# Gathering tile 1 of a product-key layer in two halves of 64 tokens

## The reference

```python
q = (xt @ wq).reshape(T, 8, 2, 128)                      # T = 256 tokens, 8 heads
scores = einsum('thcd,hcnd->thcn', q, keys)
s_top, i_top = top_k(scores, 16)                         # per half key
cand = s_top[:, :, 0, :, None] + s_top[:, :, 1, None, :]
best, pos = top_k(cand.reshape(T, 8, 256), 16)
idx  = expert number of each of the 16 best              # 128 experts for a token
gate = softmax(best)
hid  = gelu(einsum('td,thkd->thk', xt, U[idx]))          # U: 16384 x 2048
out  = einsum('thk,thkd->td', gate * hid, V[idx])        # V: 16384 x 2048
x = rms_norm(x + out)
```

## Time and profile before

| what | value |
|---|---|
| median of three runs | 2141.59 us |
| profiled execution, its time | 2130.46 us |
| its span, first to last instruction | 2128.6 us |
| gathers of U: first and last issue | 873.5 and 1541.6 us |
| tile 1's weights begin | 1555.8 us |
| last copy of the scatter ends | 1611.4 us |
| gathers of V's columns: last issue | 2101.1 us |
| busy: PE, DVE, ACT, POOL | 69%, 76%, 41%, 46% of the span |
| DMA engines in the gather stage | 0.95 to 1.02 busy, 367 to 425 GB/s |

### The profile page before, as it was taken

The page is one execution under the profiler, slowest core; times in us unless marked ns, Lnnn a source line. Parts: engine busy times, 40 slices in busy tenths (PEclk is TensorE's granted clock), DMA queues, the critical chain, the costliest instruction groups (busy, mean ns, idle before and its releaser), DMA issues.

```text
span 2128.6 us, 26462 instructions
## 1 busy us (share of the span) xinstructions
PE 1476.9 (69%) x9809; PEld 1370.3 (64%) x9809; DVE 1614.0 (76%) x2119; ACT 870.0 (41%) x1109; POOL 973.1 (46%) x699
## 2 busy tenths in 40 slices
PE   6999999999999999920000001221358999999996
PEld 6987998898999889820000001221347999999996
DVE  4455765455644556789999989877988999999997
ACT  4353432343333444312111226567655444444443
POOL 1002220000000000168888888888867777667763
PEclk9999999999999999965555555555579999999998
DMA  5555434444554555689999999999917999999996
GB/s 190 175 180 187 154 125 139 163 145 139 178 170 168 199 181 174 254 312 422 422 419 412 421 401 407 409 417 422 420 78 249 355 359 357 361 363 358 359 355 237
DMA packets 151527, 597.80 MB, mean 281 GB/s; under 512 B 14688, under 2 KB 14704, under 8 KB 118000
## 3 DMA queue, kind: packets, MB, share of 16 engines
q0 software_dynamic: 58048, 356.02, 41.8%
q1 hardware_dynamic: 93360, 240.22, 32.0%
HBM read 594.09 MB, written 2.10 MB: 280 GB/s over the span
## 4 chain that ended last, share of the span: by engine, by line
PE 50%; issue 19%; POOL 13%; DVE 12%; DMA 4%; ACT 2%; POOLq 0%; DVEq 0%; SPq 0%; ACTq 0%; PEldq 0%
PE acc L1567 8%; PE acc L1570 8%; PE acc L1569 8%; POOL slots L489 6%; POOL starts L528 5%; DVE slots L1368 4%; PE acc L1584 3%; PE acc L1586 3%; PE acc L1585 3%; DMA slots<-in_peer_u,expert 3%; PE acc L1872 2%; PE acc L1874 2%; PE scr L1874 2%; PE acc L1873 2%; PE scr L1872 2%
## 5 line engine op out<-in xcount | busy, mean ns | idle before, releaser
L857 DVE TENSOR_TENSOR w_lo<-raw,w_hi 128x2048 fp32r<-128x2048 f32 x136 | 314.7, 2314 | 311.5 <-ACT w_hi L544 310.4
L1368 DVE SCALAR_TENSOR_TENSOR slots<-slots,acc 128x2048 f32<-128x2048 f32 x188 | 424.7, 2285 | 46.3 <-DMA slots<-in_peer_u,expert 44.2
L544 ACT ACTIVATE w_hi<-raw 128x2048 fp32r<-128x2048 f32 x136 | 260.1, 1913 | 441.5 <-PE acc L1570 295.6
L528 POOL DMA_INDIRECT starts<-in_v_gather,expert x256 | 346.5, 1353 | 150.1 <-DVE X L1508 97.7
L489 POOL DMA_INDIRECT slots<-in_peer_u,expert x256 | 252.1, 985 | 257.2 <-DVE expert L1340 148.4
L1567 PE MATMUL acc<-hT_hi,w_hi 128*128 128x256 f32 x1024 | 293.9, 287 | 3.1 <-PE acc L1570 2.6
L497 POOL TENSOR_TENSOR slots<-slots,N 128x2048 f32<-128x2048 f32 x62 | 280.5, 4525 | 32.7 <-DMA slots<-in_peer_u,expert 32.4
L1569 PE MATMUL acc<-hT_lo,w_hi 128*128 128x256 f32 x1024 | 291.8, 285 | 0.0
L1570 PE MATMUL acc<-hT_hi,w_lo 128*128 128x256 f32 x1024 | 291.6, 285 | 0.0
L830 ACT ACTIVATE v_hi<-v_raw 128x1408 fp32r<-128x1408 f32 x128 | 177.0, 1383 | 278.2 <-PE scr L1874 239.0
L739 ACT ACTIVATE slots<-slots 128x2048 f32<-128x2048 f32 x62 | 118.4, 1910 | 362.4 <-POOL slots L497 362.4
(11 more groups left out here) (278 smaller groups left out, 3336.7 us busy)
## 6 DMA issues: line engine op xcount, KB each, us to landing
raw<-in_w_in SPq DMA_DIRECT2D x88, 1024.0 KB, 4.9
v_raw<-in_v_dense SPq DMA_DIRECT2D x128, 704.0 KB, 6.2
raw<-in_w_o SPq DMA_DIRECT2D x16, 1024.0 KB, 5.0
raw<-in_peer_wq SPq DMA_DIRECT2D x16, 1024.0 KB, 5.1
raw<-in_w_a_up SPq DMA_DIRECT2D x8, 1024.0 KB, 5.0
raw<-in_w_b_up SPq DMA_DIRECT2D x8, 1024.0 KB, 5.0
slots<-in_peer_u,expert POOLq DMA_INDIRECT x256, 9.4
starts<-in_v_gather,expert POOLq DMA_INDIRECT x256, 6.3
```

The costliest lines, as they stand in the source:

```text
L528: pool.indirect_dma_start(starts[s % CRING][:, :], None, v_gather[:, :], bass.IndirectOffsetOnAxis(ap=expert[:, s // NSEL, s % NSEL:s % NS ...
L544: a.activation(w_hi[:, m % 2, :, :], raw[:, m % 2, :, :], ACT.Copy).then_inc(hi_ready, 1)
L857: v.tensor_tensor(w_lo[:, m % 2, :, :], raw[:, m % 2, :, :], w_hi[:, m % 2, :, :].bitcast(fp32), ALU.subtract).then_inc(lo_ready, 1)
L1368: v.scalar_tensor_tensor(out=slots[j][:, :], in0=slots[j][:, :], scalar=1.0, in1=row, op0=ALU.mult, op1=ALU.mult, accum_out=hid_sum[:, t, ...
```

## The change

Tile 1's 128 gathers are laid out in two phases of 64 (`PHASES` = 0, 128, 192, 256). A gather of phase 1 fetches for each of the first 64 tokens of tile 1 two of its experts, one into partition p and one into partition 64 + p; phase 2 does so for the last 64 tokens. The number of gathers and their bytes stay. What goes with it:

- SP copies the expert numbers (`expert_twice`, 16 DMAs between partitions) and doubles the tokens' vectors in `N1` (three DMAs of 512 KB).
- The sums lie in two halves of the partitions; `fold_hid` on TensorE brings them to one row for a token, through PSUM.
- `rows_to_psum`, `weights`, `turn_gate` and `copy_gate` run three times in place of two.
- 48 of the 64 scatter batches lie beside the gathers (groups 35 to 63: one for a group until 42, then 40 in 21 groups), 16 behind them. Every second batch from 8 on, and the first eight, take the gate weight on ACT.
- The row ring: gather 127 goes to DVE in place of POOL; from gather 204 on the ring has seven buffers, 6, 7, 8, 11, 12, 9, 10 in this order, three of them new.
- First one-hots behind the gathers: ten places, two made by ACT in groups 60 and 61, most by POOL.

```diff
-ROW_AT = (24, 152, 32, 40, 48, 56, 64, 72, 80, 88)
-LAST_TEN = 124
+ROW_AT = (24, 152, 32, 40, 48, 56, 64, 72, 80, 88, 112, 160, 188)
+FIRST_TEN, LAST_TEN = 10, 124
+LAST_EIGHT = 204
+LATE_ROWS = (6, 7, 8, 11, 12, 9, 10)
+PHASES = (0, NSEL, NSEL + NSEL // 2, GATHERS)
+HALF = P // 2
...
+SCATTERS = NT * BATCHES
+IN_GATHERS = SCATTERS - BATCHES // 2
...
-SPREAD_FROM, SPREAD_TWICE = 35, 57
+SPREAD_FROM, SPREAD_TWICE = 35, 43
...
-    return q % FOUR == FOUR - 1 and FOUR <= q < GATHERS - 1
+    return q % FOUR == FOUR - 1 and FOUR <= q < GATHERS - 1 and q != NSEL - 1
...
     if q < LAST_TEN:
-        return (q - FOUR) % len(ROW_AT)
-    return 2 + (q - LAST_TEN) % SLOTS
+        return (q - FOUR) % FIRST_TEN
+    if q < LAST_EIGHT:
+        return 2 + (q - LAST_TEN) % SLOTS
+    return LATE_ROWS[(q - LAST_EIGHT) % len(LATE_ROWS)]
...
+def weighted_first(n):
+    return n < IN_GATHERS and (n < ACT_WEIGHTS or n % 2 == 0)
...
-    return "dve" if n % PLACES == 7 else "act" if n % PLACES == 3 else "pool"
+    return "act" if n < AHEAD or n == 12 else "dve" if n == 9 else "pool"
...
+            def double_experts(pair):
+                sp.wait_ge(expert_ready, 4 + pair + 1)
+                ks = slice(2 * pair * TOPK, 2 * (pair + 1) * TOPK)
+                cs = slice(pair * TOPK, (pair + 1) * TOPK)
+                for u in range(2):
+                    for r in range(2):
+                        sp.dma_start(expert_twice[r * HALF:(r + 1) * HALF, u, cs].rearrange("p (h k) -> p h k", h=2),
+                                     expert[u * HALF:(u + 1) * HALF, 1, ks].rearrange(
+                                         "p (h r k) -> p h r k", h=2, r=2)[:, :, r, :]).then_inc(experts_in[pair], 16)
+            double_experts(0)
+            double_experts(1)
+            sp.wait_ge(product_ready, sum(map(on_pool, range(NSEL))))
+            for r in range(2):
+                sp.dma_start(N1[r * HALF:(r + 1) * HALF, 0, :], N1[0:HALF, 1, :]).then_inc(rows_in, 16)
+            sp.wait_ge(rows_in, 32)
+            sp.dma_start(N1[0:HALF, 1, :], N1[HALF:P, 1, :]).then_inc(rows_in, 16)
+            double_experts(2)
+            double_experts(3)
...
+                if phase:
+                    act.wait_ge(rows_in, (32, 48)[phase - 1])
+                    for q in range(PHASES[phase] - SLOTS, PHASES[phase]):
                         if not on_pool(q):
                             act.wait_ge(row_used[buffer_of(q)], uses_before(q + 1, buffer_of(q)))
...
                 if i == GROUPS // 2 - 1:
                     rows_to_psum(1)
+                if i == PHASES[2] // FOUR:
+                    rows_to_psum(2)
                 if on_pool(FOUR * i + FOUR - 1):
                     sum_product(FOUR * i + FOUR - 1)
-                if i == GROUPS // 2 + 1:
-                    weight_curves(0)
+                for w in range(NT):
+                    if i == PHASES[w + 1] // FOUR + 1:
+                        weight_curves(w)
...
             def dot(q):
...
+                phase = phase_of(q)
+                if q >= FOUR and q - PHASES[phase] >= 2:
+                    dve.wait_ge(h2_rows, 2 * phase + 2)
                     row = acc[:, :, :].rearrange("p a n -> p (a n)")
+                else:
+                    if phase:
+                        dve.wait_ge(rows_in, (32, 48)[phase - 1])
+                    row = N1[:, phase // 2, :]
...
+            def fold_hid(w):
+                pe.wait_ge(ij_ready, NT)
+                pe.wait_ge(gateT_ready, w)
+                for j in range(len(ROW_AT)):
+                    if uses_before(PHASES[w + 1], j):
+                        pe.wait_ge(row_used[j], uses_before(PHASES[w + 1], j))
+                for r in range(2):
+                    rows = slice(r * HALF, (r + 1) * HALF)
+                    to = hid_ps.rearrange("p (h r k) -> p h r k", h=H, r=2)[:, :, r, :]
+                    for u in range(w):
+                        last = t_.matmul(to, (ident if u == r else turned)[rows, :],
+                                         hid_sum[rows, 1, u * HALF:(u + 1) * HALF].rearrange("p (h k) -> p h k", h=H),
+                                         start=u == 0, stop=u == w - 1)
+                    if r == 0:
+                        last.then_inc(half_folded, 1)
+                        pe.wait_ge(half_folded, w)
+                last.then_inc(hid_landed, 1)
...
-            for n in range(BATCHES):
-                scatter(0, n)
-            turn_gate(1)
-            for n in range(BATCHES):
-                scatter(1, n)
+                if m == spread(PHASES[2] // FOUR + 1)[0]:
+                    fold_hid(1)
+                    turn_gate(1)
+                scatter(m)
+            fold_hid(2)
+            turn_gate(2)
+            for m in range(IN_GATHERS, SCATTERS):
+                scatter(m)
```

More of the change, by code:

```diff
@@ L121, in spread, with until @@
 def spread(g):
-    twice = 2 * max(0, g - SPREAD_TWICE)
-    first = max(0, min(g, SPREAD_TWICE) - SPREAD_FROM) + twice
-    return range(min(BATCHES, first), min(BATCHES, first + (g >= SPREAD_FROM) + (g >= SPREAD_TWICE)))
+    def until(g):
+        late = GROUPS - SPREAD_TWICE
+        return (max(0, min(g, SPREAD_TWICE) - SPREAD_FROM)
+                + max(0, g - SPREAD_TWICE) * (IN_GATHERS - SPREAD_TWICE + SPREAD_FROM) // late)
+    return range(until(g), until(g + 1))
+def weighted_first(n):
+    return n < IN_GATHERS and (n < ACT_WEIGHTS or n % 2 == 0)
 def parts(g):
@@ L479, in gather @@
                 t, k, j = q // NSEL, q % NSEL, buffer_of(q)
-                if k % (2 * TOPK) == 0:
+                index = expert_twice[:, k // HALF, k % HALF:k % HALF + 1] if t else expert[:, 0, k:k + 1]
+                if t == 0 and k % (2 * TOPK) == 0:
                     pool.wait_ge(expert_ready, q // (2 * TOPK) + 1)
+                if t and k < HALF and k % TOPK == 0:
+                    pool.wait_ge(experts_in[k // TOPK], 64)
+                if j == 10 and not uses_before(q, j):
+                    pool.wait_ge(product_ready, sum(map(on_pool, range(PHASES[2]))))
+                if j == 12 and not uses_before(q, j):
+                    pool.wait_ge(ij_ready, NT)
                 if q == 0:
@@ L721, in _, with rows_to_psum @@
                     hi(G_WQ + 2, m, i, 4)
-            def rows_to_psum(t):
+            def rows_to_psum(phase):
                 act.wait_ge(h2_ready, NT)
-                if t:
-                    for q in range(NSEL - SLOTS, NSEL):
+                if phase:
+                    act.wait_ge(rows_in, (32, 48)[phase - 1])
+                    for q in range(PHASES[phase] - SLOTS, PHASES[phase]):
                         if not on_pool(q):
@@ L819, in high_e @@
                 q, at0 = 2 * pair // (P // PIECES), 2 * pair % (P // PIECES)
-                for t in range(NT):
-                    last = a.activation(e_hi[:, pair % 2, t, :],
-                                        weight_of[t][q][:, at0:at0 + 2, :].rearrange("p a s -> p (a s)"), ACT.Copy)
+                a.activation(e_hi[:, pair % 2, 0, :],
+                             weight_of0[q][:, at0:at0 + 2, :].rearrange("p a s -> p (a s)"), ACT.Copy)
+                last = a.activation(e_hi[:, pair % 2, 1, :].rearrange("p (a u s) -> p u a s", a=2, u=2),
+                                    weight_of1[:, :, 2 * pair:2 * pair + 2, :], ACT.Copy)
                 last.then_inc(e_hi_ready, 1)
@@ L1836, in scatter @@
+            def scatter(m):
+                pe.wait_ge(scattered, 1 + m)
+                n = m - IN_GATHERS
+                if m < IN_GATHERS:
+                    pe.wait_ge(a_ready[0], m + 1)
                 else:
                     by = maker(n)
-                    earlier = sum(maker(m) == by for m in range(PLACES, n + 1))
-                    pe.wait_ge(a_ready[("pool", "dve", "act").index(by) + 1], earlier + (PLACES if by == "act" else 0))
-                pe.wait_ge(b_hot_ready, t * BATCHES + 1 + n)
+                    pe.wait_ge(a_ready[("pool", "dve", "act").index(by) + 1],
+                               sum(maker(e) == by for e in range(n + 1)))
+                pe.wait_ge(b_hot_ready, 1 + m)
```

257 lines of the change are left out of this document (143 added, 114 removed).

## The result

| | before | after |
|---|---|---|
| median of 20 runs | 2138.54 us (2132.71 to 2146.48) | 2148.87 us (2140.9 to 2155.33) |
| profiled execution (its span) | 2130.46 us (2128.6) | 2151.72 us (2149.9) |

The ratio is 1.0041, with a 95% interval of 1.0028 to 1.0054: slower by 0.41%, 8.8 us (6.0 to 11.5 by the interval; the two medians lie 10.3 us apart). The forecast was 8.4 us faster.

A forecast was written before the change was run, and what follows sets the result against it. It took DMA as the gather stage's bound, with the scatter tail behind it wholly on the path. Terms -23.5 + 9.8 + 0.3 + 3.75 + 1.2 = -8.4 us gave a 2133 us median, range 2118 to 2150 (forecast's own 2126 to 2139).

The forecast's parts named there:

- tail's scatter: Behind the last gather: 16 of 32 scatter batches leave the tail, which gets 23.5 us shorter.
- from product 251 to it: Between POOL's last product and the tail's scatter: fold_hid replaces the softmax part at about equal cost, difference 0.
- phase 2 begins: Around gather 204: ACT's late copy to PSUM delays DVE, then POOL, and DMA loses 9.8 us (ends 2 and 16).
- ring of seven: Late gathers: buffer reuse waits for ACT's sum with 0.7 us left; cost 0 to 2 us, taken as 0.3.
- copies of the vectors: Gather stage: three copies of 512 KB between partitions at 412 GB/s add 3.75 us of DMA time.
- tile 1 begins: Gathers 123 to 131: late doubled vectors, gather 127 on DVE, a freer dot 128; taken 0, ends -1 and +4.
- expert numbers: Gather stage: 16 DMAs in 2048 pieces of 32 B add 1.2 us; ready some 15 us before they are wanted.
- the weights before it cost the same: Before the tail's scatter: softmax part (1.55 us) goes, fold_hid (taken as 1.6 us) comes; ends -0.4 and +1.
- the distance of four: Ring at phase 2: gather 204 reuses gather 200's buffer, formerly eight apart; 7.4 us lost at gather 204.
- rival C: Vector copies touching 64 partitions run at half rate, 7.5 us in place of 3.75; total 2137 us; chance 0.15.
- A (lateness hidden): Phase 2's start: the lateness mostly doesn't reach DMA, 2 of 9.8 us stay; total 2125 us; chance 0.24.
- B (the handshake as bound): Groups from 43: ACT, TensorE and DVE wait on each other, groups outlast DMA's 10 us; 2154 us; chance 0.17.

The follow-up runs named there:

- e4: Changed kernel with the 40 later scatter batches one group earlier, in groups 43 to 62, none behind the last dot: 2146.7 us, ratio 1.0022 to the kernel before.
- e2: Changed kernel with the late ring's order 11, 12, 10, 6, 7, 8, 9, its unused buffers first: 2141.36 us, ratio 0.9998 to the kernel before.
- e3: Changed kernel with phase 2's copy to PSUM ahead of ACT's scatter work of group 47: 2150.93 us, ratio 1.0052 to the kernel before.
- e1: Changed kernel without the three copies of the tokens' vectors (tile 1's vectors then wrong): 2141.48 us, ratio 1.0001 to the kernel before.
- e5: Changed kernel with its three vector copies replaced by copies of the same bytes over all 128 partitions (vectors wrong): 2140.86 us, ratio 1.0006 to the kernel before.
- e8: The kernel before, unchanged, executed again for a second profile ("before again" in the table): 2149.95 us.
- e7: Changed kernel with new buffers first in the ring, the early copy to PSUM and later batches in groups 43 to 62: 2139.28 us, ratio 0.9991 to the kernel before.

## Why the prediction was wrong

| step | predicted | measured |
|---|---|---|
| tail's scatter | -23.5 | -24.8 |
| from product 251 to it | 0 | +5.0 |
| phase 2 begins, ring of seven | +9.8, +0.3 | +16.2 |
| copies of the vectors, tile 1 begins | +3.75, 0 | +9.1 |
| expert numbers (131 to 187) | +1.2 | +1.5 |
| tile 0 (11 to 123; +1.3 in before again) | 0 | +1.8 |
| sum | -8.4 | +8.8 |

Of the 17.2 us between -8.4 and +8.8, phase 2 makes 6.1, the copies 5.3 and the queue before the tail 5.0; the rest is small and partly noise.

*Tail, right.* 16 batches went, and half of 51.2 would have been 25.6; the measured 24.8 lies between that and the 23.5. TensorE's granted clock was no different: its mean is 0.88 over the 28 us of the tail after and over the first 27.8 us of the tail before.

*From the last product to the tail, wrong: the queue was not counted.* The text priced `fold_hid` at 1.6, and that is what e4 leaves. The failed step is "the weights before it cost the same": in TensorE's program group 63's batch stands ahead of the fold, its product ran until 1596.47, and the fold began then. 3.4 us, shown by e4.

*Phase 2, mechanism right, size short by 6.1.* The place, dot 194's wait (7.5 forecast, 6.24 seen), POOL's wait (11.7 late, 12.85 seen) and the distance of four are as forecast, and e2 confirms the last. So is the main term, 7.4 us without data at gather 204: the windows from 1445 to 1455 show 8.0. What failed is what stands around it. The text has no loss before gather 204, and the stretch 187 to 199 already lost 3.1. There the issues of two gathers beside the dots that read `N1` took 2.85 and 1.88 us in place of 0.95, and DMA was 0.81 busy from 1420 to 1425. Behind it the text had 1.6 and 0.8 more; 199 to 207 took 12.5 us longer than before and 207 to 251 0.5, so 5 us beside the 8.0. Over the 60 us from 1420 DMA moved 19.2 MB, 13.3 us less than at 412 GB/s. Part of the rest is a rate of 357 to 392 GB/s at shares of 0.97 to 1.00 from 1425 to 1440, and no run shows why. The fix that I would have drawn from my own text, e3, gained nothing, for the exp behind it was as late; I had listed the weights' length and not what ACT's part of them is queued behind.

*Copies, wrong.* The failed step is "Three copies of 512 KB at 412 GB/s". They cost 11.3 us (e1; 10 by the other runs), at full width 3.7 (e5). This is rival C's cause, to which I gave 0.15, and its 7.5 us were too little as well. The trace shows why: the gathers in flight beside them slowed down with them, to 218 GB/s in their own time, where e5 has 418. The sign that I had named for it, a gather stage longer by over 5 us where tile 1 begins, is the one that came. The lower end of -1 for tile 1's begin was real: without copies (e1) the stretch is 2.2 us shorter than before, and the net is +9.1. The missing product 127 fits: dot 128 took 2.29 us in e1 and in the kernel after, with no product beside it, against 4.17. No run tests it by itself.

The Trainium skill (SBUF — State Buffer, "Door 1: The DMA port swizzle") says that a transfer gets the ports that its partitions reach, half of them for 0 to 63. The runs agree: 29.9 and 31.2 us with 64 partitions from either source, 23.6 with 128. I should have given the rule more weight than a row's silence: no row contradicted it.

*Expert numbers, size not to be told, reason wrong.* POOL did wait for them. The 15 us that I had called plenty were under 10: the last numbers were ready at 1356.15 and POOL wanted them at 1365.93. SP issued the last four copies at 1356.18, and the gather that needs them reads:

```profile
1356.18 2.54 SPq L433 DMA_DIRECT2D expert_twice<-expert  x4
...
1368.97 0.97 POOL L539 DMA_INDIRECT slots<-in_peer_u,expert_twice  x1 [3.04 <-DMA expert_twice<-expert]
```

That is over 10 us from the last issue, for 4 KB each. The stretch's sum is within what e8 varies by.

*Rivals.* A (lateness hidden) is refuted by the 0.60 of 1440 to 1460. B (the handshake as bound) is refuted too: from 207 to 251 the groups took 110.5 us for eleven, 10.05 each, in after, 10.0 in before. B would have needed 10.3 or more.

*The range.* The measured median of 2148.87 us lies inside my 2118 to 2150, but by luck: the upper end was drawn for B, which didn't happen, and my own forecast's range ended at 2139.

*What stays open.* e7 gained 11.5 us in place of 13 to 16, which the intervals can't tell from the sum of its parts (13.3 us by the ratios of e2 and e4); phase 2's last 6.7 us, and its rate below 412 GB/s at a share near 1; and the variation of the stages ahead of and behind the gathers, which e8 shows but nothing explains.

## What to carry to other kernels

Where DMA is the bound, count partitions as well as bytes: here a transfer into half of the partitions slowed the others in flight too, and an idle TensorE that moved the data through PSUM was the cheaper way (10 to 11 us against 0.2). When work is moved, look at what stands ahead of each step in its engine's queue, on every engine the step touches, and beyond the first wait to the next: taking away one of two waits in a row gained nothing. At a change of a ring's order, work out the distance for each of the first buffers, and put the unused ones there.

## What the runs showed of the hardware

- A DMA share near 1 is not a rate: 0.98 to 1.02 of busy time went with 210 to 233 GB/s beside copies into 64 partitions, and with 407 to 426 beside copies into 128. The longest landing of an indirect gather was 25.2 us beside the former, 17.7 beside the latter (e5), 15.5 without copies (e1) and 13.9 in the kernel before.
- Where phase 2 begins, two issues of indirect gathers beside dots with two SBUF inputs took 2.85 and 1.88 us, against a median of 0.95; so they did in the kernel before where tile 1 begins. The first of those dots took 4.16 us, with POOL's product beside it as well; the second, beside the issues alone, took 2.28, as others do.
- Beside the gathers, the copies of 512 KB landed in 8.7 to 14.8 us, and four copies of 4 KB took over 10 us as well: a small copy there wasn't a quick one.
- One kernel's stage ahead of the gathers and the dense stage differed by 5.8 and 7.3 us between two executions, 0.6% of the time, more than the change itself makes.
